# Output projection of a hybrid encoder layer: each tile is transposed one product sooner

## The reference

```python
x = layer_norm(x, ln_emb_g, ln_emb_b)
proj = x @ w_in                       # split into u, q, k, v
heads = concatenate([fourier_mix(u, w_fourier), windowed_attention(q, k, v, sink_logits)])
x = layer_norm(ALPHA * x + heads @ w_out, ln_mix_g, ln_mix_b)      # output projection
h = square(relu(x @ w_ff1))
x = layer_norm(ALPHA * x + h @ w_ff2, ln_ffn_g, ln_ffn_b)
```

## Time and profile before

| | |
|---|---|
| median of 3 runs | 2452.34 us (2450.99 to 2452.35) |
| the profiled execution | 2452.33 us, its span 2450.7 us |
| PE busy | 2376.5 us, 97% of the span |
| DVE busy | 1579.2 us, 64% |
| ACT busy | 1090.4 us, 44% |
| DMA | 547.76 MB, mean 224 GB/s |
| mean granted PE clock | 0.987 of full speed |

### The profile page before, as it was taken

The page is one execution under the profiler, slowest core; times in us unless marked ns, Lnnn a source line. Parts: engine busy times, 40 slices in busy tenths (PEclk is TensorE's granted clock), DMA queues, the critical chain, the costliest instruction groups (busy, mean ns, idle before and its releaser), DMA issues. The chain is left out here.

```text
span 2450.7 us, 35017 instructions
## 1 busy us (share of the span) xinstructions
PE 2376.5 (97%) x12038; PEld 2073.4 (85%) x12038; DVE 1579.2 (64%) x2214; ACT 1090.4 (44%) x1774; POOL 180.8 (7%) x245
## 2 busy tenths in 40 slices
PE   6999998999999979999999999999999999999998
PEld 5888887999788768888899989998888888888886
DVE  8655366666666676666666666666455596668667
ACT  3111146887211154444655565555433344444442
POOL 1000001211222200000000000000000010001001
PEclk9999999999999989999999999999999999999999
DMA  7766776322356665555766776668766669777974
GB/s 270 288 263 233 271 208 219 79 68 86 122 199 239 261 266 194 208 210 217 279 228 243 242 284 228 241 238 305 260 196 192 189 212 335 226 219 254 307 225 135
DMA packets 220313, 547.76 MB, mean 224 GB/s; under 512 B 21672, under 2 KB 90920, under 8 KB 200620
## 3 DMA queue, kind: packets, MB, share of 16 engines
q1 hardware_dynamic: 204128, 488.19, 57.2%
q0 software_dynamic: 16080, 58.20, 7.2%
HBM read 365.95 MB, written 180.36 MB: 223 GB/s over the span
## 5 line engine op out<-in xcount | busy, mean ns | idle before, releaser
L65 PE MATMUL e_bank<-e_hi,e_lo 128*128 128x512 f32 x1120 | 435.8, 389 | 0.4 <-DVE e_lo L2165 0.4
L67 PE MATMUL e_bank<-e_hi 128*128 128x512 f32 x1120 | 435.7, 389 | 0.0
L66 PE MATMUL e_bank<-e_lo,e_hi 128*128 128x512 f32 x1120 | 435.7, 389 | 0.0
L65 PE MATMUL u_bank<-u_x_hi,u_wa_lo 128*128 128x384 f32 (+1 forms) x768 | 272.5, 355 | 5.3 <-DVE u_wa_lo L1769 2.0
L67 PE MATMUL u_bank<-u_x_hi,u_wa_hi 128*128 128x384 f32 (+1 forms) x768 | 271.9, 354 | 0.0
L2165 DVE TENSOR_TENSOR e_lo<-e_raw,e_hi 128x896 fp32r<-128x896 f32 (+1 forms) x168 | 189.3, 1135 | 120.2 <-ACT e_hi L2136 119.5
L2136 ACT CAST e_hi<-e_raw 128x896 fp32r<-128x896 f32 (+1 forms) x168 | 165.2, 983 | 209.4 <-PE e_bank L67 195.8
L65 PEld LDWEIGHTS e_bank<-e_hi,e_lo 128*128 128x128 f32 x1120 | 210.2, 188 | 44.9 <-DVE e_lo L2165 1.2
L67 PEld LDWEIGHTS e_bank<-e_hi 128*128 128x128 f32 x1120 | 210.2, 188 | 43.7
L66 PEld LDWEIGHTS e_bank<-e_lo,e_hi 128*128 128x128 f32 x1120 | 210.2, 188 | 43.5
L65 PE MATMUL u_bank<-u_x_hi,u_wb_lo 128*128 128x384 f32 (+1 forms) x576 | 205.0, 356 | 9.1 <-DVE u_x_rest L1746 9.1
(11 more groups left out here) (277 smaller groups left out, 4526.6 us busy)
## 6 DMA issues: line engine op xcount, KB each, us to landing
u_w_sum<-s_ws SPq DMA_DIRECT2D x34, 1024.0 KB, 4.8
c_vt_raw<-w_ff SPq DMA_DIRECT2D x24, 1024.0 KB, 7.9
c_q_raw<-w_ff SPq DMA_DIRECT2D x24, 1024.0 KB, 7.8
s_h<-c_k_raw SPq DMA_DIRECT2D x32, 768.0 KB, 6.9
e_raw<-s_t SPq DMA_DIRECT2D x96, 256.0 KB, 3.7
e_raw<-s_h SPq DMA_DIRECT2D x112, 192.0 KB, 2.8
ab_place<-w_ff SPq DMA_DIRECT2D x18, 1024.0 KB, 8.7
s_h<-c_k_raw SPq DMA_DIRECT2D x96, 192.0 KB, 2.2
```

Source lines behind the costliest of these rows:

```text
L65: tensor.matmul(out, w_lo, m_hi, start=first, stop=False, skip_group_check=again)
L66: tensor.matmul(out, w_hi, m_lo, start=False, stop=False, skip_group_check=again)
L67: return tensor.matmul(out, w_hi, m_hi, start=False, stop=last, skip_group_check=again)
```

## The change

PE now runs transpose n - 1 behind product n, from n = 1 on, and one transpose is left for the end. DVE calls `mix_quarters(n // 2 - 1)` after each even norm from n = 2 on, and one at the end. SP waits for and stores pair n // 2 - 1 after the `x1` store of each even n from 2 on, where it did so for odd n from 3 on. Nothing is computed in another way, and no buffer changes.

```diff
             for n in range(NT):
                 sp.wait_ge(x1_done, n + 1)
                 sp.dma_start(x1_d[mix_rows(n), :], x1[:, n % 2, :]).then_inc(x1_st[n % 2], 16)
-                if n % 2 and n > 2:
+                if n % 2 == 0 and n:
                     q = n // 2 - 1
                     sp.wait_ge(mixed_done, q + 1)
                     sp.dma_start(xb_d[q], mixed[:, q % 2, :, :]).then_inc(mixed_st[q % 2], 16)
...
-                if n % 2 == 0 and n >= 4:
-                    mix_quarters(n // 2 - 2)
-            mix_quarters(NT // 2 - 2)
+                if n % 2 == 0 and n:
+                    mix_quarters(n // 2 - 1)
             mix_quarters(NT // 2 - 1)
...
             product(0)
-            product(1)
-            for n in range(2, NT):
+            for n in range(1, NT):
                 product(n)
-                transpose(n - 2)
-            transpose(NT - 2)
+                transpose(n - 1)
             transpose(NT - 1)
```

## The result

The changed kernel takes 2458.82 us (median of 9 runs, 2455.00 to 2460.64), the kernel before 2452.35 us (9 runs, 2450.90 to 2453.53). The ratio is 1.0027 with a 95% interval of 1.0017 to 1.0037: slower by 0.27%, 6.5 us. The profiled execution took 2458.49 us, with a span of 2456.8 us.

The account below looks back on a forecast made before the run. PE, busy 97% of the span, bounds the kernel, so only its waits and clock count. Transposes +0.9, block's end -2.0, stall +4.6 and clock +2.5 give +6.0 on 2452.33: 2458.3 us, range 2451 to 2461 (forecast's own 2455.3 to 2460.4).

Parts of the forecast that it names:

- the end of the block: Output projection's end: last pair stored 0.75 us sooner, engines meet 2.0 sooner, MLP's `s_ws` load follows; 2.0 us gained.
- the sum: Whole kernel: -1.1 (transposes' shift less the shorter end) + 4.6 (stall) + 2.5 (clock) = +6.0 us.
- The transposes: Output projection: each product from 2 on starts 0.89 us later, with `x1` ready 5.5 us in hand; +0.9 us.
- The delay of the heads: Tile 16's heads land 6.3 us later, behind early MLP weights and `x1` of tile 14; bounds 0 and 7.5.
- The stall: PE waits for `h_lo` before product 16, 4.6 us (0 to 5.8).
- No second stall: After product 16: norm 15 has `x1` ready near 820.7, before product 16 ends at 822.7.
- The clock: Behind the stall at product 16, PE's granted clock falls to the lower level, costing 2.5 us; bounds 0 and 3.4.
- The rule on sharing: DMA queues with work take turns, a packet each, so the weights take turns among the packets of tile 16's heads.
- Rival 2: At tile 16's heads: q1's newcomers wait until q0 has drained, no stall, 2451.2 us; chance 14%.
- the lower bound of 0.75: Start of the MLP: the load from `s_ws` comes sooner by at least what the last store gains, 0.75 us.
- the bound of 4.9 us: Whole kernel: about 0.2%, the smallest difference from no change that a measurement of this kernel can tell.

Follow-up runs that it names:

- run 23: Not a run's label but a verb: product 16 runs 23 matmuls in the changed kernel with 20 filling matmuls ahead of its wait for `h_lo`; 2456.88 us.

## Why the prediction was right, step by step

The time of 2458.82 lies 0.5 us from the forecast of 2458.3. The mechanism that makes the kernel slower was right in each link. The gain at the end of the block was not, and that the sum comes so close is in part luck: what this term had too much, other stages gave back.

- **The transposes.** Predicted +0.9, and no product waiting for `x1`. The kernel with the transposes alone shows 0.87 us in its trace and no wait.
- **The delay of the heads.** Predicted 6.3 us by bytes, issue to landing from 12.4 to 18.7; it was 18.7. The weights alone were predicted at 5.1 and made 5.1. That bytes by rate is only a rough rule shows in the kernel with one weight load early, 4.7 instead of 3.8.
- **The stall.** Predicted 4.6 us, measured 4.46, PE's own row says 4.21. No second stall followed, as worked out.
- **The clock.** Predicted 2.5; the profiled execution lost 2.5, and filling the stall gave back 1.9 in the median, 1.5 by the ratios. The bounds were needed: one profiled execution with 3.06 us of waiting lost nothing.
- **The rule on sharing.** From 797 to 804 the queues of the changed kernel had equal packets and unequal bytes:

```profile
q1 hardware_dynamic: 274, 1.95, 66.1%
q0 software_dynamic: 270, 1.03, 35.9%
```

By the Trainium skill (DMA: Bandwidth & Descriptors, Queues, rings and completion order) the queues take turns by packets: this trace agrees, 274 to 270, if the packets that the profile counts are those of the page. Rival 2, that the newcomer waits till q0 has drained, held only for the start: nearly nothing of q1 moved until 794, some 4 us after its issue.

- **The end of the block.** This step failed: "it follows by at least what the store gains, 0.75, and at most 2.0". The meeting did come 2.0 us sooner, counted from the end of product 19. But ACT had the load from `s_ws` only at 884.47, 8.74 us later than before, where `x1` of the last tile was 8.99 us later: 0.25 gained, not 2.0, and less than the lower bound of 0.75.

```profile
884.47 1.04 ACT L1861 CAST u_wa_hi<-u_w_sum 128x1024 fp32r<-128x1024 f32 x1 [5.04 <-DMA u_w_sum<-s_ws]
```

What I overlooked is that before, pair 8's store was moving when the last one was issued. One window each, before and then after, is the microsecond from the issue of the last store (PEclk, DMA share and GB/s are the last three columns):

```profile
865.70:866.70 1.00, 0.00 (x0) 0.00 (x0) 0.00 (x0) 0.00 (x0) 0.00 (x0) 0.50 1.07 459
```

```profile
873.90:874.90 1.00, 0.09 (x1) 0.12 (x1) 0.01 (x1) 0.11 (x1) 0.00 (x0) 0.50 0.50 215
```

Before, one store follows the other without a gap, at 459 GB/s. In the changed kernel the last store is alone: its first bytes move at 874.75, 0.8 us after the issue, and from 875 to 876 the rate is again 459 GB/s. The store lands 7.2 us after its issue (7.0 before), and the load 3.3 us behind the store (3.0 before). Of the 0.77 us by which the store goes out sooner, some 0.25 reach the load. Why the load falls back another 0.3 us behind the store is not shown. The kernel with the split store shows that the load depends on the store ahead of it.

So the stage cost +0.9 - 0.25 + 4.46 + 2.5 = +7.6 in the profiled execution against the +6.0 of the sum. Another 1.1 us had been lost ahead of this stage, and yet the whole time was only 6.2 us longer. Some 2.6 us were gained in the MLP (PE's matmuls come 8.75 us later than before near 1000 us, and 6.15 near 1500), for the most part where two stretches at 1.2 GHz, near 1214 and 1446 us, were 3.4 us long in this execution and 6.8 us, near 1203 and 1448, in that of before. Neither is in the sum. The two kernels with the same end of the block and no stall agree on the size of the failed term: counted from the stage's first matmul, PE goes on behind its wait for `u_wa_lo` 0.55 us later than before with late weights, and 0.59 later with POOL's loads moved away, and not 1.1 sooner. The runs scatter over 2.6 us before and 5.6 us in the changed kernel; whether such stretches make this scatter was not traced, so their share in the median stays open.

The chances of slower and no change were put at 0.48 each; the median is beyond the bound of 4.9 us, while the single runs reach down to 2455.0.

## What to carry to other kernels

When a list that issues transfers is reordered, look first at what its waits were holding back: a wait that seems to be only about its own buffer can be what keeps a large prefetch out of another one's way. Weigh each load not by its size but by its margin, the time between its landing and its first use, and by all bytes ahead of it in both queues; a move of the same bytes behind the load that is needed next cost nothing. And a meeting of engines that comes sooner is worth only what the first load behind it gains, here 0.25 of 2.0 us.

## What the runs showed of the hardware

- A queue that started while another one kept the 16 DMA engines busy for 0.84 to 0.95 of the time (790 to 794) moved its first bytes 3 to 4 us after issue (790.3 to about 794), and then shared packet for packet. With packets of 8 KB against 4 KB it got two thirds of the bytes. The last store of the block, alone, moved its first bytes 0.8 us after issue.
- The same wait of PE doesn't always cost the clock: 2.03 us of waiting were followed by 3.4 us at 1.2 GHz before, and 2.7 us by as much in the kernel with one weight load early, but 3.06 us by none in one execution of the kernel with the weights forward. So these executions give no length of a wait from which on the clock falls.
- Matmuls whose result nobody reads paid twice: 20 in the stall let product 16 run 23 matmuls instead of 12 in 4.9 us, and 22 before the last transposes brought 0.88 us in the trace: the eight transposes took 1.09 us instead of 1.97, and everything behind the store followed.
